# Expert slots kept by block of 128 tokens: four 32-slot column tiles, rows gathered for four expert pairs at once, outputs turned back from 64 rows

## The reference, cut to what matters

```python
def hier_moe(x, w_group, b_group, w_inner, b_inner, w_gate, w_up, w_down):
    ...
    gates = jnp.sum(jax.nn.one_hot(eidx, N_EXPERTS, dtype=jnp.float32) * weight[..., None], axis=-2)
    h = (jax.nn.silu(jnp.einsum('btd,edf->btef', x, w_gate))
         * jnp.einsum('btd,edf->btef', x, w_up))
    h = h * gates.astype(h.dtype)[..., None]
    return jnp.einsum('btef,efd->btd', h, w_down)
```

## Time and profile before

| what | value |
|---|---|
| median of three runs (lowest, highest) | 688.43 us (686.83, 689.33) |
| profiled execution: span from first to last instruction | 686.9 us |
| mean granted TensorE clock over the span | 0.979 of full speed |
| busy: TensorE / VectorE / ScalarE / GpSimd | 629.0 / 363.6 / 262.6 / 96.8 us |
| moved from HBM | 143.11 MB read, 1.05 MB written |

### The profile page before, as it was taken

One profiled execution on the slowest core, in us unless ns is written; L12 is line 12 of the kernel. 1 busy time (PEld: TensorE's weight loads), 2 busy tenths in 40 slices (PEclk: granted clock), 3 DMA queues, 4 the chain that ended last, 5 costly groups with the idle time before them and its releaser, 6 DMA issues. The chain is left out here.

```text
span 686.9 us, 13967 instructions
## 1 busy us (share of the span) xinstructions
PE 629.0 (92%) x6047; PEld 432.9 (63%) x6047; DVE 363.6 (53%) x585; ACT 262.6 (38%) x384; POOL 96.8 (14%) x128
## 2 busy tenths in 40 slices
PE   4999979989989879899999989999979989999994
PEld 4775857868868767544444359997757754444432
DVE  4894987834566586412323476587644641233236
ACT  5464642443253424231112345566643432112112
POOL 6970055040033030000000000012120000000000
PEclk9999989999999999999999999999999999999998
DMA  8952442200000138999999732543301999999911
GB/s 314 275 199 66 149 157 89 101 4 5 4 4 5 63 142 320 410 409 409 410 408 409 297 126 84 164 135 128 105 1 64 411 408 409 409 410 409 408 72 63
DMA packets 48643, 145.16 MB, mean 211 GB/s; under 512 B 4808, under 2 KB 4976, under 8 KB 48576
## 3 DMA queue, kind: packets, MB, share of 16 engines
q1 hardware_dynamic: 47696, 142.28, 54.9%
q0 software_dynamic: 880, 1.91, 1.0%
HBM read 143.11 MB, written 1.05 MB: 210 GB/s over the span
## 5 line engine op out<-in xcount | busy, mean ns | idle before, releaser
L1169 DVE TENSOR_TENSOR w_lo<-w_ring,w_hi 128x2048 fp32r<-128x2048 f32 x32 | 75.6, 2369 | 22.0 <-PE ps L1863 11.9
L708 ACT ACTIVATE w_hi<-w_ring 128x2048 fp32r<-128x2048 f32 x32 | 60.8, 1909 | 53.4 <-PE ps L1863 30.6
L1861 PE MATMUL ps<-w_hi,xa_hi 128*128 128x512 f32 x128 | 53.3, 417 | 11.6 <-issue 5.2
L1356 DVE SCALAR_TENSOR_TENSOR hact_s<-silu_s,slot_gates,ps 128x256 f32<-128x256 f32 x16 | 7.7, 480 | 104.8 <-issue 76.5
L1862 PE MATMUL ps<-w_lo,xa_hi 128*128 128x512 f32 x128 | 52.1, 407 | 0.0
L1863 PE MATMUL ps<-w_hi,xa_lo 128*128 128x512 f32 x128 | 52.0, 406 | 0.0
L679 POOL TENSOR_TENSOR att<-att,causal 128x256 f32<-128x256 f32 x16 | 14.9, 950 | 257.9 <-ACT att L1105 257.9
L2402 PE MATMUL ps<-load,xe 128*64 128x512 f32 x192 | 43.3, 597 | 4.2 <-ACT xe L813 2.6
L2415 PE MATMUL ps<-load,hs 128*64 128x512 f32 x192 | 43.3, 593 | 0.5 <-DVE y_lo L1362 0.4
L2402 PE MATMUL ps<-load,xT 128*64 128x512 f32 x192 | 43.7, 608 | 0.0
L822 ACT ACTIVATE silu_s<-ps,slot_gates 128x256 f32<-128x256 f32 x16 | 7.6, 472 | 91.9 <-issue 81.3
(11 more groups left out here) (369 smaller groups left out, 1407.6 us busy)
## 6 DMA issues: line engine op xcount, KB each, us to landing
load<-in_moe_w_gate_dram SPq DMA_DIRECT2D x48, 512.0 KB, 11.7
load<-in_moe_w_up_dram SPq DMA_DIRECT2D x48, 512.0 KB, 12.8
load<-in_moe_w_down_dram SPq DMA_DIRECT2D x48, 512.0 KB, 14.0
w_ring<-in_rw_w_rkv_dram SPq DMA_DIRECT2D x24, 512.0 KB, 6.5
w_ring<-in_moe_w_gate_dram SPq DMA_DIRECT2D x16, 512.0 KB, 12.2
w_ring<-in_moe_w_up_dram SPq DMA_DIRECT2D x16, 512.0 KB, 13.3
w_ring<-in_moe_w_down_dram SPq DMA_DIRECT2D x16, 512.0 KB, 12.0
w_ring<-in_w_kv_dram SPq DMA_DIRECT2D x16, 512.0 KB, 5.1
```

The lines of the kernel that those rows point to most:

```text
L708: nc.scalar.activation(whi[n % HI][:, :, :], w_ring[n % RING][:, :, :], ACT.Copy).then_inc(hi_ready, 1)
L1169: nc.vector.tensor_tensor(wlo[n % LO][:, :, :], w_ring[n % RING][:, :, :], whi[n % HI][:, :, :].bitcast(f32), ALU.subtract).then_inc(lo_re ...
L1861: nc.tensor.matmul(dst, xh, wh, start=start, stop=False)
```

## The change

Slots are given out by expert and token block: 32 for each of the two blocks, so an expert has 64 as before, and a block's tokens stand in rows of their own. A pair's 128 slots are four column tiles in the order (block 0, first expert), (block 0, second), (block 1, first), (block 1, second). With that:

- places are counted within a block (four small matmuls for five); the branch to `all_experts` is taken when some expert has more than 32 tokens of one block;
- one `gather` call serves four pairs and two channel blocks, and a token block is multiplied by its own slots alone: 2 x 2 x 2 = 8 matmuls of 256 columns. There are eight calls per mixture: numbers 0 and 1 ahead of the branch, 2 ahead of the first `gate_up`, 3 between its halves, 4 to 7 around the halves of p = 3. Calls 0 and 2 wait for the low parts of the tokens' first and second half of the channels;
- `gate_up` and `down` issue four matmuls of 32 slots where two of 64 stood, each with the same 512 moving columns;
- `gather_gates` becomes four float32 matmuls of 32 slots by 4 columns, and moves: for p = 0 from ahead of the second half to behind it, for later pairs ahead of `down`;
- `combine` takes 64 slots of one token block at a time (rows 0 to 63 for j = 0, 64 to 127 for j = 1), into four banks instead of two; `combine_rows` is one step;
- gates are no longer split in two parts, `slot_gates` is one copy, `pick_t` has 128 columns instead of 256.

The calls of `next_dense` and the loads are as before.

```diff
-    SLOTS = P // 2
+    CAP = P // 4
+    SLOTS = NT * CAP
     NP = E // 2
+    GP = 4
...
+        OUT_BANK = ((6, 7), (2, 3))
+        GATHERS = [((2, 3), (0, 1)), ((6, 7), (2, 3)), ((0, 1), (4, 5)), ((2, 3), (6, 7)),
+                   ((2, 3), (0, 1)), ((6, 7), (2, 3)), ((2, 3), (4, 5)), ((6, 7), (6, 7))]
...
-                with pe.If(most < SLOTS + 1):
+                with pe.If(most < CAP + 1):
...
+            def gather(k, n):
+
+                banks, blocks = GATHERS[n]
+                pe.wait_ge(packed_sems[k]["pick"], n // 4 + 1)
+                for bank, b in zip(banks, blocks):
+                    dst = PS[:, bank, :].rearrange("p (q j x) -> p q j x", q=GP, j=NT)
                     for part, x_ in enumerate((xt_hi, xt_lo)):
...
+                        if n in (0, 2) and b == blocks[0]:
+                            pe.wait_ge(moe_sems[("xt_hi", "xt_lo")[part]], k * PER["xt_lo"] + NT * (n // 2 + 1))
                         for j in range(NT):
...
+                            m = nc.tensor.matmul(dst[:, :, j, :], x_[:, j, b * P:(b + 1) * P],
+                                                 pick[n // 4][:, j, :].rearrange("p (q x) -> p q x", q=GP),
+                                                 start=j + part == 0, stop=j + part == 2)
...
-                        for c in range(2):
-                            m = nc.tensor.matmul(PS[rows(c), 4, :].rearrange("p (a f) -> p a f", a=2),
-                                                 xe[q % 2][:, b, c0 + c * SLOTS:c0 + (c + 1) * SLOTS], w[c][:, i, :, :],
+                        for j, c, o in TILES:
+                            m = nc.tensor.matmul(PS[o, 4, :].rearrange("p (a f) -> p a f", a=2),
+                                                 xe[:, b, c0 + o.start:c0 + o.stop], w[c][:, i, :, :],
...
+                        for j in range(NT):
+                            o = slice(2 * CAP * j, 2 * CAP * (j + 1))
+                            m = nc.tensor.matmul(PS[:, OUT_BANK[j][a], :], pick_t[p % 3][o, :], y_[o, a, :],
+                                                 start=first and part == 0, stop=last and part == 1)
...
+                gather(k, 2)
                 for p in range(NP):
                     more = p < NP - 1
                     gate_up(p, 0)
                     if p == 0:
-                        gather(k, 0, 1)
-                        pe.wait_ge(moe_sems["gates_parts"], k * PER["gates_parts"] + 1)
+                        pe.wait_ge(s["x_dve"], 1)
+                        gather(k, 3)
+                    if p == GP - 1:
+                        gather_next(4)
+                        gather_next(5)
+                    gate_up(p, 1)
+                    if p == 0:
+                        pe.wait_ge(moe_sems["gates"], k * PER["gates"] + 1)
                         gather_gates(0)
```

More of the change, by code:

```diff
@@ L185, in trunk_program @@
         lg = mplace("lg", [P, NT, NR])
-        gates = mplace("gates", [P, NT, 2 * E + 2])
+        gates = mplace("gates", [P, NT, E, 4])
         r_gs = mplace("r_gs", [P, NT, G])
@@ L368, in trunk_program @@
         PER = dict(xT_act=2, xT_dve=2, lgT_psum=1, lgT=1, logits=1, gate_args=2, gate_exps=2, chosen=1, places=1, n_max=1,
-                   xt_hi=2 * NT, xt_lo=2 * NT, gates_parts=1, ffn_row=16)
+                   xt_hi=2 * NT, xt_lo=2 * NT, gates=1, ffn_row=16)
         moe_sems = {q: sem(f"moe_{q}") for q in PER}
@@ L784, in moe_phase @@
                 most = act.value_load(n_max_int[0:1, 0:1])
-                with act.If(most < SLOTS + 1):
+                with act.If(most < CAP + 1):
                     packed_experts(k)
@@ L1264, in moe_phase @@
                 linked = steps[0]
-                with dve.If(most < SLOTS + 1):
+                with dve.If(most < CAP + 1):
                     packed_experts(k)
@@ L1390, in packed_experts @@
                         gates_out(p + 1)
-                    if p % 2 and p + 3 < NP:
-                        pick_pairs(k, (p + 3) // 2)
+                    if p == GP - 1:
+                        channels(7)
                     if p:
@@ L1420, in all_experts @@
                 gate_weights(k)
+                dve.wait_ge(moe_sems["gates"], k * PER["gates"] + 1)
                 for p in range(NP):
@@ L2373, in packed_experts @@
                 s = packed_sems[k]
-                def rows(c):
-                    return slice(c * SLOTS, (c + 1) * SLOTS)
+                TILES = [(j, c, slice((2 * j + c) * CAP, (2 * j + c + 1) * CAP)) for j in range(NT) for c in range(2)]
                 def gather_gates(p):
@@ L2413, in down @@
                         for f in range(NF):
-                            for c in range(2):
-                                m = nc.tensor.matmul(PS[rows(c), a, :], hs[:, f, rows(c)], w[c][:, f, a, :],
+                            for j, c, o in TILES:
+                                m = nc.tensor.matmul(PS[o, a, :], hs[:, f, o], w[c][:, f, a, :],
                                                      start=f == 0, stop=f == NF - 1)
@@ L2456, in packed_experts @@
                     if more:
-                        gather_gates(p + 1)
+                        pe.wait_ge(s["gates_out"], p + 2)
                     turn(p)
+                    if p == GP - 1:
+                        pe.wait_ge(*X_READY[1][2])
+                        pe.wait_ge(*X_READY[1][3])
                     if p >= 2:
-                        combine_rows(p - 2, 0)
-                    if p + 2 < NP:
-                        gather(k, p // 2 + 1, p % 2)
-                    if p >= 2:
-                        combine_rows(p - 2, 1, 6 if more else 2)
+                        combine_rows(p - 2)
                 down(NP - 1)
-                for j in range(NT):
-                    pe.wait_ge(s["added"], 4 * (NP - 3) + 2 * j + 2)
-                    for a in range(2):
-                        combine(NP - 2, j, a, (2 if j else 6) + a, last=False)
+                pe.wait_ge(s["added"], 4 * (NP - 2))
+                for a in range(2):
+                    combine(NP - 2, a, last=False)
+                pe.wait_ge(s["pick_t"], NP)
                 for a in range(2):
                     pe.wait_ge(s["y_lo"], 2 * NP - 1 + a)
-                    for j in range(NT):
-                        combine(NP - 1, j, a, (2 if j else 6) + a, first=False)
+                    combine(NP - 1, a, first=False)
             def all_experts(k):
```

196 lines of the change are left out of this document (92 added, 104 removed).

## The result

The changed kernel took **669.13 us** (median of four runs, 667.87 to 671.24), the kernel before, run beside it, 688.13: a ratio of 0.972, 95% interval 0.969 to 0.975. Forecast was 667, with 660 to 677 as the range.

A forecast was written before the change was run, and what follows sets the result against it. The prediction took moe1's pairs as bound by TensorE, only just ahead of the weight loads. Terms of -14.4 (moe1) and -7.1 (moe0) took the 686.9 us span to 665.4; plus 1.5 for the median, 667 us, range 660 to 677.

The forecast's parts named there:

- Banks: moe1, before p = 7: four banks end combine's 1.34 us wait for VectorE's add, -1.3 us.
- Start: Start of moe1: first gate_up later (+1.7), less between its halves (-2.3), turn later behind gate_up (+0.9), net +0.3 us.
- Gates: Gates matmuls in each moe1 pair: 0.55 becomes 0.45 us, -0.6 over six pairs.
- the loads would cap moe1 at about -15.5, with 1 to 2 us to spare: End of moe1: the last weight load, landing at about 654 to 655, would still arrive before TensorE reads it.
- moe0, -7.1 forecast: End of moe0: splits of attention pieces ahead of silu(7) and gated(7) wait for landing; -7.1 us, between -9.5 and -5.
- the landing: End of moe0: the attention pieces' last 2.0 MB land at 385.2 us, by bytes through the queue; TensorE idles 6.6 us.
- the clock: TensorE behind moe0's wait: 4 us at half clock; the last down, 3.65 us, loses 0.8.
- Tail: End of each mixture: 16 combine matmuls behind the last down run two by two, -0.8 us.
- Four tiles below full rate: Rival for gate_up and down: a 512-column round takes 1.07 instead of 0.88 us, 697 us in all; chance 0.08.
- Row halves in turn: Rival for combine: the two row halves do not run together, 676 us in all; chance 0.12.
- moe0 does not wait: Rival for moe0's end: no wait for the splits, so moe0 also gives 14.4 us, 660 us in all; chance 0.05.
- all_experts: Rival for the branch: all_experts is taken, 56 us more per pair, over 1300 us in all; chance under 0.01.

The follow-up runs named there:

- light_down1: The changed kernel with only the first 256 of 1024 columns of each w_down loaded in moe1, same TensorE work: 664.10 us.
- after_again: The changed kernel, nothing edited, measured and profiled a second time: 667.92 us.
- tiles_serial: The changed kernel with gate_up issuing all four matmuls of a half on one column tile, then the next tile, instead of tiles in turn: 798.97 us.
- splits_late: The changed kernel with the first attention pieces' splits moved from ahead of silu(7) and gated(7) to behind moe0's last y_hi and last add: 662.31 us.
- before_splits_late: The kernel before the change, with the same move of the splits as splits_late: 693.28 us, ratio 1.006.
- pieces_later: splits_late with the loads of attention pieces 2 and 3 issued after moe0's last add: 669.29 us.
- combine_serial: The changed kernel with combine's matmuls (p = 0 to 5) ordered all four of token block 0, then all four of block 1: 667.06 us.
- splits_late_2: pieces_later with w_hi of piece 2 and w_lo of piece 1 also moved behind the attention's first set of normed channels: 658.10 us.

## Why the prediction was right, point by point

**moe1, -14.4 forecast: -13.5 and -14.4 measured.** The sum held, by two errors that cancel. Gathers, combine (1.1 forecast, 1.12 measured), the pair at p = 3 (near 17; 579.74 to 596.48 by gate_up's starts, 16.74) came as worked out, the 1.34 us wait of the step "Banks" is gone, and the first gate_up started 1.5 us later from the router, against the 1.7 of the step "Start" (whose net was -0.8 against +0.3: the first turn comes 21.1 us after the router, before 21.9). But the pair is 12.0, not 12.6: the step "Gates" took 0.45 where the chain shows 0.05, and the 0.35 us gap ahead of combine, which I left in, went. Against that, "the loads would cap moe1 at about -15.5, with 1 to 2 us to spare" was too mild, as the faster pair reached the cap: two waits for weights, which the prediction had listed as a sign of being wrong, and a half clock behind the second. light_down1 prices all of it at about 5 us.

**moe0, -7.1 forecast: -2.9 and -5.4 measured.** The mechanism was right in every link: splits ahead of silu(7), pieces that land late, a wait released by hact, a half clock. Two terms were mis-sized, and the first profile lies outside the bounds that the prediction gave, -9.5 and -5. First the landing: counted from the router, I had piece 1 at 116.9 us (385.2 less 268.3) and its split started at 118.9 (383.18 less 264.3). The change did not move it: in the kernel before, the last of the pieces' four transfers, issued at 375.4, landed 11.7 us later, at 387.1, which is 118.9 us from the router too:

```profile
L63 SPq DMA_DIRECT2D w_ring<-in_w_kv_dram x4: 379/695/1016, 373.4 to 375.4; - x4
...
DMA to landing us min/median/max: 9.3/10.5/11.7
```

So my count of bytes through the queue was 2 us short in the kernel before already: by that landing the weights' queue had moved 48.9 MB (q1, from 265.4 us on), where I counted 48.2. The 0.7 MB more are 1.8 us at 387 GB/s; that they are packets of the pieces issued behind is likely, but I did not follow it up. Second the clock: I priced 4 us at half speed, and in the first profile it stayed at half until 394, so that the last down took 5.42 us; in after_again 3.99. In the first profile it fell once more behind that, and the transposes took 3.63 us instead of 1.97. The wait itself, 11.5 us against 6.6, cost nothing beyond that: TensorE only arrived earlier, with 12.0 us pairs, at a landing that stands 118.9 us behind the router either way.

"Tail", -0.8, came in moe1 (0.9 to 1.0 less from last down to the end) and hardly in moe0, where VectorE's four adds follow the last combine either way: 5.0 us from last down to transposes, before and after.

**The rivals.** *Four tiles below full rate*: excluded, 3.64 us a half against 3.65. The Trainium skill (TensorE: Matmul & The Clock Gate, Part 3) has measured speedups of 3.07 for four row tiles and 2.38 for three column tiles. Here, in a stream of 32 records, it is 4.0: in tiles_serial a record of one tile alone takes 0.43 us (303.41 to 303.84), and four tiles in turn take 3.64 us for 32 records, four in every 0.43 us. One tile behind the other, tiles_serial, halved that. *Row halves in turn*: excluded, 1.12 us. *moe0 does not wait*: excluded in the changed kernel, and realised by splits_late, which lost half of the gain again to the next thing in line. *all_experts*: not taken.

**The total**, -21.5 forecast, was -20.4 in the first profile. By stage that is -16.4 in the mixtures and -4.0 of luck ahead of them; in after_again -19.8 and -2.1. So the change's own part is 16 to 20 us by these two profiles (the medians, -19.0 and -20.3, hold the spread of the time-mixing phase as well). That the first profile's span came within 1.1 us of the forecast was in part luck.

## What to carry to other kernels

When a stage gets shorter, look for work of the *next* stage that was put into its instruction streams because it was free there: here four splits cost nothing while TensorE covered them (before_splits_late) and 11.5 us of waiting once it did not. Every such instruction is a wait for a landing that stands ahead of whatever is behind it on that engine, and pieces_later shows how easily one is left behind. Compare profiles stage by stage from an instruction that both have, not by their spans: here one phase outside the change moves by 5 us on its own.

## What the runs showed of the hardware that I had not expected

Matmuls on different tiles overtake each other in the instruction stream: past three earlier ones in combine_serial and tiles_serial, in the second also across the border of two halves. The Trainium skill (TensorE: Matmul & The Clock Gate, Part 3) has matmuls start and end strictly in program order; these two traces disagree, and the time of combine_serial (1.12 us in either order) with them.

The clock is not a fixed price of an idle time. Behind 2.78 us of idle TensorE in the changed kernel the transposes took 3.63 us at half clock, behind 2.62 us in after_again 1.97 us at full (2.64 us in pieces_later: 1.97; 2.65 us in splits_late_2: 2.51). What decided between the two was not tried.

TensorE started the attention 3.6 us behind the last add while weight transfers filled the queue (splits_late), and 0.7 us behind it when the later pieces were held back; each time a 16 KB instruction packet had ended 1.5 us ahead of the start. The changed kernel has the same 1.5 us (399.39 to 400.87).
